# Head norm: the reciprocal of the root moved from VectorE to GpSimd, as a power of minus one

## The reference, cut to what matters

```
qa, ka, va, qi, ki, wi, qb, kb, vb, ga, gb = split_cols(h @ w_in)
"qa": rope(rms_norm(qa.reshape(b, t, H_A, HEAD_DIM), q_norm_a), pos)
"ka": rope(rms_norm(ka...), k_norm_a), "qb": ... q_norm_b, "kb": ... k_norm_b
rms_norm(x, g) = x * rsqrt(mean(x * x) + 1e-6) * g
"qi", "ki": rope without a norm; "va", "vb", "wi": neither
```

## Time and profile before

| | |
|---|---|
| median of 2 runs | 657.34 us (655.72 and 658.95) |
| the profiled execution | 658.87 us, its span 657.2 us |
| busy, share of the span | TensorE 98%, VectorE 65%, ScalarE 46%, GpSimd 24% |
| transfers | 103.05 MB, mean 157 GB/s |
| the chain that ended last | TensorE 88%, VectorE 5%, ScalarE 2%, GpSimd 1% |

### The profile page before, as it was taken

The page is one execution under the profiler, slowest core; times in us unless marked ns, Lnnn a source line. Parts: engine busy times, 40 slices in busy tenths (PEclk is TensorE's granted clock), DMA queues, the critical chain, the costliest instruction groups (busy, mean ns, idle before and its releaser), DMA issues.

```text
span 657.2 us, 12957 instructions
## 1 busy us (share of the span) xinstructions
PE 642.0 (98%) x4798; PEld 619.0 (94%) x4798; DVE 425.7 (65%) x657; ACT 299.7 (46%) x489; POOL 157.6 (24%) x220
## 2 busy tenths in 40 slices
PE   8799999999999999998999999999999999999998
PEld 5799999999999999876889889999999999999998
DVE  6666565666555568899896855986666565665441
ACT  7534444344344434546543557645535344444330
POOL 1577775000011216446521210062000000000000
PEclk9799999999999999999997999999999999999999
DMA  8576766545555453422322222554354545446530
GB/s 329 203 223 214 242 207 221 161 150 172 182 165 165 161 189 126 141 88 87 105 98 65 98 97 77 179 196 161 129 169 152 184 145 183 157 147 209 157 123 19
DMA packets 31978, 103.05 MB, mean 157 GB/s; under 512 B 5120, under 2 KB 5824, under 8 KB 31936
## 3 DMA queue, kind: packets, MB, share of 16 engines
q1 hardware_dynamic: 27504, 96.22, 44.1%
q0 software_dynamic: 3616, 4.73, 2.6%
q10 hardware_dynamic: 816, 1.54, 0.6%
HBM read 100.77 MB, written 1.70 MB: 156 GB/s over the span
## 4 chain that ended last, share of the span: by engine, by line
PE 88%; DVE 5%; ACT 2%; issue 2%; POOL 1%; DMA 1%; ACTq 0%; SPq 0%; DVEq 0%; POOLq 0%
PE ps L1103 27%; PE ps L1105 27%; PE ps L1104 27%; DVE roots L1022 1%; DVE wlo L796 1%; DVE acc L960 1%; POOL act_tmp L474 1%; PE ps L1293 1%; DMA x<-in_x 1%; PE ps L1279 1%; PE ps L1216 1%; ACT whi L555 1%; PE ps L1248 1%; PE ps L1330 1%; PE ps L1125 0%
## 5 line engine op out<-in xcount | busy, mean ns | idle before, releaser
L796 DVE TENSOR_TENSOR wlo<-raw,whi 128x1024 fp32r<-128x1024 f32 (+1 forms) x181 | 228.6, 1267 | 121.3 <-ACT whi L555 121.1
L1103 PE MATMUL ps<-nhi,whi 128*128 128x288 f32 x952 | 288.6, 303 | 2.4 <-DVE nlo L822 2.4
L1104 PE MATMUL ps<-nlo,whi 128*128 128x288 f32 x952 | 282.4, 297 | 0.0
L1105 PE MATMUL ps<-nhi,wlo 128*128 128x288 f32 x952 | 281.4, 296 | 0.0
L555 ACT ACTIVATE whi<-raw 128x1024 fp32r<-128x1024 f32 (+1 forms) x181 | 182.4, 1030 | 138.6 <-PE ps L1105 130.7
L1103 PEld LDWEIGHTS ps<-nhi,whi 128*128 128x128 f32 x952 | 179.8, 189 | 7.6 <-issue 5.1
L1104 PEld LDWEIGHTS ps<-nlo,whi 128*128 128x128 f32 x952 | 180.0, 189 | 0.8
L1105 PEld LDWEIGHTS ps<-nhi,wlo 128*128 128x128 f32 x952 | 180.3, 189 | 0.0
L1103 PE MATMUL ps<-hhi,whi 128*128 128x288 f32 x336 | 99.5, 296 | 0.0
L1104 PE MATMUL ps<-hlo,whi 128*128 128x288 f32 x336 | 99.1, 295 | 0.0
L1105 PE MATMUL ps<-hhi,wlo 128*128 128x288 f32 x336 | 98.8, 294 | 0.0
(11 more groups left out here) (181 smaller groups left out, 706.8 us busy)
## 6 DMA issues: line engine op xcount, KB each, us to landing
raw<-in_weights SPq DMA_DIRECT2D x166, 512.0 KB, 3.4
raw<-in_weights SPq DMA_DIRECT2D x16, 384.0 KB, 3.6
kt<-in_cache_kidx_a POOLq DMA_DIRECT2D x32, 32.0 KB, 2.6
kt<-in_cache_k_b POOLq DMA_DIRECT2D x16, 64.0 KB, 3.4
kt<-in_cache_k_a POOLq DMA_DIRECT2D x32, 32.0 KB, 3.2
vb_pg<-in_cache_v_b POOLq DMA_DIRECT2D x16, 64.0 KB, 3.3
cst<-in_constants ACTq DMA_DIRECT2D x1, 980.0 KB, 8.1
x<-in_x SPq DMA_DIRECT2D x2, 288.0 KB, 4.0
```

The lines of the kernel that those rows point to most:

```text
L796: nc.vector.tensor_tensor(wlo[:, v % NU, 0:nk, 0:w], raw[:, v % NR, 0:nk, 0:w], whi[:, v % NU, 0:nk, 0:w].bitcast(F32), ALU.subtract).then ...
L1103: nc.tensor.matmul(out[0:w, 0:N], h, hi, start=start and i == 0, stop=False)
L1104: nc.tensor.matmul(out[0:w, 0:N], h, lo, start=False, stop=False)
L1105: ins = nc.tensor.matmul(out[0:w, 0:N], l, hi, start=False, stop=stop and done is not False and i == len(ks) - 1)
```

## The change

VectorE no longer takes the reciprocal. GpSimd waits for the root itself, raises `roots` in place to the power of a column that holds -1.0, signals itself, and multiplies as before. The column is a new memset of VectorE at the start, with a semaphore of its own.

```
+            nc.vector.memset(eps_col[:, 3:4], -1.0).then_inc(minus_one, 1)
...
                 if u - 1 in NORMED:            # GpSimd
                     i = index_among(u - 1, NORMED)
                     pool.wait_ge(zg_ready, i + 1)
+                    pool.wait_ge(zroot_ready, i + 1)
+                    if i == 0:
+                        pool.wait_ge(minus_one, 1)
+                    nc.gpsimd.tensor_tensor(roots[:, i % 2, :], roots[:, i % 2, :], eps_col[:, 3:4].to_broadcast([P, N]), ALU.pow)\
+                        .then_inc(zrstd_ready, 1)
                     pool.wait_ge(zrstd_ready, i + 1)
                     nc.gpsimd.tensor_tensor(zloc[u - 1], zloc[u - 1], roots[:, i % 2, :], ALU.mult).then_inc(zn_ready, 1)
...
-                if u - 1 in NORMED:            # VectorE
-                    i = index_among(u - 1, NORMED)
-                    dve.wait_ge(zroot_ready, i + 1)
-                    nc.vector.reciprocal(roots[:, i % 2, :], roots[:, i % 2, :]).then_inc(zrstd_ready, 1)
```

More of the change, by code:

```diff
@@ L316, in build @@
         x_in = [sem(f"x_in{i}") for i in range(len(X_PARTS))]
-        scaled_gains, masks_ready, warm_ready = [sem(s) for s in "scaled_gains masks_ready warm_ready".split()]
+        scaled_gains, masks_ready, warm_ready, minus_one = [sem(s) for s in "scaled_gains masks_ready warm_ready minus_one".split()]
         (squares_ready, ms_done, root_ready, n_hi, n_lo) = [sem(s) for s in
```

## The result

| | before | after |
|---|---|---|
| median of 2 runs | 657.34 us | 1085.49 us (1084.91 and 1086.06) |
| the profiled execution | 658.87, span 657.2 | 1086.06, span 1084.4 |
| busy, TensorE / VectorE / GpSimd | 642 / 426 / 158 us | 664 / 402 / 611 us |

The ratio is 1.651, with a 95% interval of 1.644 to 1.658. The forecast was 719.5 us in a range of 652 to 830: the direction is right, the size is wrong by a factor of nearly seven, and the time lies outside the range.

What follows compares the result with a forecast made beforehand. TensorE bounds the kernel overall, VectorE's list slots 12 to 16. With X the power's length, 658.9 + (7X - 3.8) + (X - 1.9) + (2X - 5.7) = 647.5 + 10X: 719.5 us at 7.2, range 652 to 830.

Steps and rivals of the forecast that it cites:

- Added: the power, X us each: GpSimd's new power in ten head norms, X its length: taken as 7.2 us from 16 estimated steps of 0.45 us.
- The upper end of 40 steps: Longest length allowed for one GpSimd power: a careful form with 40 estimated steps, 18.1 us, giving a kernel of 828.5 us.
- third rival: GpSimd's power is far longer, over 12 us, as dependent steps: kernel from 768 us up, no upper end from rows; chance 0.19.
- What a long GpSimd instruction blocks: Each GpSimd power was to hold up VectorE's splits and accumulations for its whole length, extrapolated from products of 0.81 us.
- second rival: The power does not hold VectorE up, GpSimd alone makes the ring: 18.3 us instead of 40.6, 697 us; chance 0.10.
- 647.5 + 10 X: Forecast kernel time in us for a power over 3 us with VectorE held up; 719.5 with a power of 7.2.
- The ring and its factor of ten: Slots 11 to 17: seven powers and 40.6 us between them, taking turns; with three other powers, ten power lengths are added.
- Removed: at most 8.45 us: Five of ten VectorE reciprocals, in slots 12 to 16, stand on the chain; at most 8.45 us leave it.
- The cover of 3.1 us in slot 5: Before unit 4's swap, 3.1 us of slot 5's power are hidden behind TensorE, which waits for the rest.
- The stretch behind the last swap: The part of the kernel after 325 us was to keep its length.
- TensorE's clock: In longer pauses it might fall to 1.2 GHz; a unit then takes about twice 3.4 us, hidden in a slot of 11.7.
- no new wait: GpSimd's wait for the root was to come at no cost, as the reciprocal had waited for it already.

Runs made afterwards that it cites:

- experiment 4: Against the kernel before, only the sixth head norm (unit 12, slot 13) takes GpSimd's power, the nine others keep VectorE's reciprocal: 698.75 us against 655.98.
- experiment 5: The changed kernel with a GpSimd product of 128 x 1440 into a scratch tile in place of each power, no reciprocal: 665.97 us.
- experiment 8: The changed kernel with the power taken on only 16 of 288 columns: 660.22 us against 658.83 for the kernel before, ratio 1.004.
- experiment 1: The kernel before with the head norms' reciprocal left out and nothing in its place, GpSimd multiplying by the root: 653.29 us against 655.98, ratio 0.995.
- experiment 9: The kernel before with ScalarE's inverse root replacing root and reciprocal in head norms and the three norms of x: 653.23 us against 657.50, ratio 0.993.
- experiment 10: The kernel before with ScalarE's inverse root in the ten head norms alone, norms of x unchanged: 653.46 us against 658.83, ratio 0.993.
- experiment 3: Against the kernel before, only the first head norm (unit 4, slot 5) takes GpSimd's power, the nine others keep VectorE's reciprocal: 700.65 us against 655.98.

## Why the prediction was wrong

- **The step "Added: the power, X us each"** failed. X was taken as 7.2 us (16 steps of 0.45), between 0.8 and 18.1; it is 46.2, as long as 102 such steps. The sum has ten times X, so this one term is 390 us, more than the 366 missed; the step below takes 22 of them back. The upper end of 40 steps was no bound at all: no row of the kernel before showed any GpSimd operation but products, additions and copies, and the number of steps was invented. The third rival said that a row could give no upper end; the range should have followed it.
- **The step "What a long GpSimd instruction blocks"** failed for the power and held for the product (experiments 4, 5 and 8). The rows at 0.8 us were read rightly, but carried over to another operation. This was the second rival's case: 625.2 + 10 X. With the measured X of 46.3 it gives 1088 us, and 1085.5 was measured; my forecast's 647.5 + 10 X gives 1110. So the outcome is the second rival's ring with the third rival's length, a pair which the prediction kept apart.
- **The ring and its factor of ten** held: slope 10 between 144 and 288 columns, one power 43 to 45 us dearer. The second rival's constant of 625.2 held for long powers only. With a short power GpSimd's own products wait for VectorE's splits, and it comes out at 629 (with the mean power of 3.15 us) to 631 (with the median of 2.94) (experiment 8).
- **"Removed: at most 8.45 us"** held as a bound; 2.2 to 2.7 us are to be had at equal granted clock, 2.7 to 5.4 by the medians (experiments 1, 9 and 10), since the accumulations, relu and logits are late next. So in slots 12 to 16 VectorE's list was less alone in setting the pace than the prediction had it.
- **The cover of 3.1 us in slot 5** held: experiment 3 gave 700.65 for 702 expected, and the 1.35 us between them lay in front of the power. The stretch behind the last swap kept its length too, as forecast.
- **TensorE's clock** fell to 1.2 GHz in the pauses, which I had allowed for as hidden. It was, but for slot 10: there the root came late, and GpSimd, whose wait for the root was to be "no new wait", stood 3.47 us, some 3 of them by the clock. The stretch behind the last product is not longer than before.

## What to carry to other kernels

An operation that no row shows on an engine can't be priced by its neighbours on that engine: here a factor of 58 lay between a product and a power of the same shape. Two short runs of the operation alone, on few columns, give its price per column (0.159 us here). That price, times the columns, times the ten uses that follow one another, is nearly the whole answer. A piece on the chain of waits bounds what its removal can bring; here some 2.5 of 8.45 us came.

## What the runs showed of the hardware

- GpSimd's power of two tensors costs 0.159 us a column and 0.39 fixed: 46.23 us for 288 columns, 23.31 for 144, 2.94 for 16. It is the same for 128 partitions and for 1, and for exponents of -1 and 1. What it does in that time was not looked into.
- A GpSimd product holds a two-tile VectorE instruction up until it ends (2.59 us, split 2.53 instead of 1.22). The power, a two-tensor instruction too, doesn't, short or long (splits of 1.22 and 1.23 us inside powers of 2.9 and 46.2 us), though it waits itself for a split that is under way (3.88 instead of 2.91, 46.79 instead of 46.23). Why it lets go is open.
- ScalarE's inverse root with a bias lasts 0.49 us for 128x288, as its root does.
